# When GpSimd makes the activation sums of the first feed-forward: four blocks at the hidden factors, or six portions after the additions

## The chip, the cores and the metric

One core of one Trainium2 chip runs the program. The metric is device time in microseconds. A core has TensorE (matmuls into PSUM), VectorE, ScalarE, GpSimd and SyncE (here it issues the DMAs); they run their own instruction streams and wait for each other by semaphores.

## The reference

One layer of a diffusion backbone on 1152 tokens (1024 latent and 128 context), width 1024: a half-step SwiGLU feed-forward, a token mixer, and a second feed-forward, each modulated and closed by a layer norm. The change is in the first feed-forward:

```python
def swiglu(h, w_up, w_down):
    a, u = jnp.split(h @ w_up, 2, axis=-1)
    return (jax.nn.silu(a) * u) @ w_down
...
x = layer_norm(ALPHA * x + 0.5 * g1 * swiglu(x * (1.0 + sc1) + sh1, w_f1_in, w_f1_out), ln_g[0], ln_b[0])
```

`w_up` is 1024 x 5632, `w_down` 2816 x 1024, all in float32. The modulation of the later sub-layers (`silu(c) @ w_mod + b_mod`) is worked out beside this feed-forward.

## The kernel before

**Tiling.** The hidden width of 2816 is 22 blocks of 128, taken in 11 groups of two. Every float32 operand is split in two float16 parts, hi and lo, and a product is three matmuls (`PASSES`). For group i TensorE makes six up-projections (`up(i, b, c)`: block b, token chunk c of 384, 48 matmuls each), and between the third and the fourth of them it makes the down-projection of the group before (`down(i - 1)`: 9 token tiles by 2 halves of 512 columns, 6 matmuls each). The down-projection goes through three PSUM banks, which VectorE empties by adding into Y (`add`, 18 additions in a group, counted by the semaphore `y_added`, which begins at 3).

**VectorE's order in a group** (`first_group` of the vector block): the maximum of a weight block; three modulation steps (`mod.steps`, L379, a multiply and sum over a 128 x 1024 tile); `product(i, par, 0, 0)`; `hidden_scale(i - 1)`, whose last instruction L2779 writes the hidden factor and raises `h_scale`; the scale of a weight block; `hidden_lo` (L2787, six pieces of h_lo); `win_lo` (L2730); two steps; two more products; `win_scale`; then the nine tiles of `add(i - 1, t)`, each followed by a step; then `win_lo(2i + 2)`, `wout_scale`, `product(i, par, 1, 0)`, `wout_lo` (L2755, two), two steps, a product, `win_max`, two steps, a product, `hidden_max`. At the end of group 4 it also works over the finished modulation columns (`late_columns`); groups 5 and 6 have a short late scale ahead of the additions. At the end of group 6 `halve_gates` lets TensorE turn the gates into rows (`turn_rows`, L333), ahead of group 7.

**ScalarE** makes the hi parts: after `gate(i, 0, 2)` stands `win_hi(2i + 2)`, and behind it `gate(i, 1, 0)` (the silu of the fourth up-projection) and `wout_hi`.

**Groups 7 and 8** are made otherwise: a product of half size is saved by sums of the activations and of the weights (class `Quarters`). GpSimd makes both. `Quarters.sums(gp, k, late)` makes the activation sums of one k out of four: 17 instructions on tiles of 128 x 576, each waiting for the one before (`link`), into places that stay as they are until group 8. Before the change GpSimd begins with k when `h_scale` has reached k + 2, so one block of 17 runs from the hidden factor in each of the groups 2, 3, 4 and 5. Then come the weight sums (`weight_sums`, L2036, L2039, L2042), one set for each of the blocks 14 to 17. Those of block 14 wait for its load, which SyncE issues when group 5 has split block 12 and its place is free. `win_hi(14)`, on ScalarE in group 6, waits for them (`w_summed`), since L2042 writes into the raw weights; `win_lo(14)` on VectorE (`quarter_lo`, L2722 and L2718), the first instruction after group 6's additions, waits for ScalarE. TensorE asks for the activation sums (`quarters.made`) from the fifth product of group 7 on.

Of the kernel before, what the change touches and what calls it, by code (L numbers as in the profile page):

```python
# [71 lines left out]
class Plan:  # L72


    def __init__(self, nc, base):
        self.nc, self.at = nc, base
# [1451 lines left out]
class MixOut:  # L1528
# [151 lines left out]
    def sums(self, dve, t):  # L1680

        nc, Y = self.nc, self.K.Y
        dve.wait_ge(self.y_taken, 2 * t + 2)
        nc.vector.tensor_tensor(Y[:, t, :], Y[:, t, :], self.xs[t % 2][:], ALU.add).then_inc(self.res_used, 1)
        dve.wait_ge(self.res_used, t + 1)
        if t:
            dve.wait_ge(self.bn, t)
        for half in range(2):
            self.link(nc.vector.bn_stats(self.st[:, half, :], Y[:, t, half * 512:(half + 1) * 512]))
        nc.vector.bn_aggr(self.mv[:, t, :], self.st[:]).then_inc(self.bn, 1)  # L1690
# [250 lines left out]
class Quarters:  # L1941
# [3 lines left out]
    ORDER = ((1, 0), (1, 1), (2, 0), (2, 1), (6, 0), (6, 1), (5, 0), (7, 0), (5, 1), (7, 1), (4, 0), (3, 0), (4, 1), (3, 1))  # L1945
    PER = len(ORDER)
    TMP = 4 * 3 * HALF

    def __init__(self, K, nc, tag, first_group, end_group, spots, staging_at, late_tmp_at, parts_at):
        self.K, self.nc = K, nc  # L1950
# [39 lines left out]

        return self.PER * self.number(blk) + self.at[p, c] + 1

    def sums(self, gp, k, late):

        nc, K, H = self.nc, self.K, self.HALF
        t0, t1, t2 = (t[:] for t in self.tmp[late])
        hi, lo = K.A

        def link(ins):
            self.steps += 1  # L2000
            ins.then_inc(self.summed, 1)
            gp.wait_ge(self.summed, self.steps)

        def add(out, a, b):
            link(nc.gpsimd.tensor_tensor(out, a, b, ALU.add))

        def take(out, a, b):
            link(nc.gpsimd.tensor_tensor(out, a, b, ALU.subtract))

        def split(j, k, x):  # L2010
            link(nc.gpsimd.tensor_copy(self.S[j][0][k][:], x))
            take(self.S[j][1][k][:], x, self.S[j][0][k][:])

        add(t0, hi[:, k, H:], lo[:, k, H:])
        add(t1, hi[:, self.KH + k, H:], lo[:, self.KH + k, H:])
        take(t1, t1, t0)
        split(1, k, t1)
        add(t2, hi[:, k, 0:H], lo[:, k, 0:H])
        take(t0, t2, t0)
        split(3, k, t0)  # L2020
        add(t1, t1, t2)
        link(nc.gpsimd.tensor_scalar(t0, t1, -1.0, None, ALU.mult))
        split(2, k, t0)
        add(t2, hi[:, self.KH + k, 0:H], lo[:, self.KH + k, 0:H])
        take(t1, t1, t2)
        split(4, k, t1)
        gp.sem_inc(self.made, 1)

    def weight_sums(self, gp, blk, raw, raw_in, w_max, in_lo):

        nc, n = self.nc, self.number(blk)
        four = raw[:].rearrange("p s (h k) n -> p (s h) (k n)", h=2)
        gp.wait_ge(raw_in, 32 * (blk // 2) + 32)
        if n:
            gp.wait_ge(in_lo, blk)
        nc.gpsimd.tensor_tensor(self.staged[:, 0:3:2, :], four[:, 0:4:3, :], four[:, 2:3, :].broadcast_to([P, 2, self.KH * P]),  # L2036
                                ALU.add).then_inc(self.w_chain, 1)
        gp.wait_ge(self.w_chain, 2 * n + 1)
        nc.gpsimd.tensor_tensor(self.staged[:, 1, :], four[:, 3, :], self.staged[:, 0, :], ALU.add).then_inc(self.w_chain, 1)  # L2039
        gp.wait_ge(self.w_chain, 2 * n + 2)  # L2040
        gp.wait_ge(w_max, blk + 1)
        nc.gpsimd.tensor_tensor(four[:, 2, :], self.staged[:, 1, :], four[:, 1, :], ALU.add).then_inc(self.w_summed, 1)  # L2042
# [17 lines left out]
def ffn_phase(nc, K, place, banks, tag, w_in, w_out, unit_i, first=False, out_dst=None):  # L2060

    with ExitStack() as ctx:
# [22 lines left out]
        if first:  # L2085
# [3 lines left out]
            quarters = Quarters(K, nc, tag, 7, 9, ((sums_at, sums_at + 36864), (at + 6144, at + 8448)), tmp_at, tmp_at,  # L2089
                                (tmp_at + 6144, at))  # L2090
# [3 lines left out]
        else:  # L2094
            end = Ending(K, nc, tag, place, 2, 8, out_dst, spare_at)
            mix = MixOut(K, nc, place, banks, wout_at, odd_at, odd_at + 4 * GB * TOK, end.gated_at, end.gated_at - 8192)
            quarters = Quarters(K, nc, tag, 3, NG - 1, ((end.gated_at + 12288, end.gated_at + 16384), (end.rows_at, end.rows_at + 8192),
                                                              (mix.free_at + 16384, nc.sbuf_usable_end), (mix.free_at, mix.free_at + 8192), (mix.free_at + 8192, mix.free_at + 16384)),
                                spare_at, spare_at, (end.gated_at, end.gated_at + 6144))
# [8 lines left out]
        h_max, h_spread, h_scale = sem("h_max"), sem("h_max_spread"), sem("h_scaled")  # L2108
        y_ready, y_added, chain = sem("y_ready"), sem("y_added"), sem("chain")
# [4 lines left out]
        HPG = 2 * NT  # L2114
# [579 lines left out]
        def _(dve):  # L2694
# [19 lines left out]
            def quarter_lo(blk, sums):  # L2714
                q, par = quarters, blk % 2
                if sums:
                    dve.wait_ge(q.w_hi, q.number(blk) + 1)
                    nc.vector.scalar_tensor_tensor(q.parts[par][1][:], q.staged[:], ws[:, par:par + 1], q.parts[par][0][:],  # L2718
                                                   ALU.mult, ALU.subtract).then_inc(in_lo, 1)
                else:  # L2720
                    dve.wait_ge(in_hi, blk + 1)
                    nc.vector.scalar_tensor_tensor(win[par][1][:], wraw[par][:], ws[:, par:par + 1], win[par][0][:], ALU.mult, ALU.subtract)  # L2722
# [400 lines left out]
        @block.gpsimd  # L3123
        def _(gp):
            if mod:
                mod.constants(gp)
                weight_sums = lambda blk: quarters.weight_sums(gp, blk, wraw[blk % 2], raw_in[blk % 2], w_max, in_lo)
                gp.wait_ge(mod.feed.lo, NCH * KT)
                for k in range(quarters.KH):
                    gp.wait_ge(h_scale, k + 2)  # L3130
                    quarters.sums(gp, k, False)
                for blk in range(quarters.first_block, quarters.first_block + quarters.blocks):
                    weight_sums(blk)
                gp.wait_ge(quarters.products, quarters.PER * quarters.blocks)
                qkv.pool(gp)
                att.pool(gp)
            else:
                K.tail.root(gp)
                mix.pool(gp)
                gp.wait_ge(mix.feeds[0].lo, 2 * KT)  # L3140
                gp.wait_ge(mix.feeds[1].lo, KT)
                for k in range(quarters.KH):
                    if k == quarters.KH - 1:
                        gp.wait_ge(mix.y_taken, 2 * NT)
                    quarters.sums(gp, k, False)
                gp.wait_ge(mix.scaled_rows, 2)
                for blk in range(quarters.first_block, GB * (NG - 1)):
                    quarters.weight_sums(gp, blk, wraw[blk % 2], raw_in[blk % 2], w_max, in_lo)
                    n = 3 * ((blk - quarters.first_block) // GB)
                    if n < pieces.COUNT:  # L3150
                        pieces.affine(gp, *((n + 1, n + 2) if blk % 2 else (n,)))
                end.pool(gp, y_added, (NG - 2) * HPG + 3)
# [6 lines left out]
def hgrn_phase(nc, K, place, banks):  # L3159

    with ExitStack() as ctx:
# [33 lines left out]
        (raw_in, w_hi, w_lo, acc_p, left, lbs, ready, head) = (  # L3195
            sem(n) for n in ("w_loaded", "w_hi", "w_lo", "projected", "left_psum", "lb_ready", "consts_ready", "head_cols"))
        (logf, sums, sums_e, dev, e_dev, factors) = (
            sem(n) for n in ("logf", "sums", "sums_exp", "deviation", "deviation_exp", "factors"))
        (kt_s, kb_s, a_s, am_s, u_s, st_s, o_s, oe_s) = (
# [348 lines left out]
        def _(act):  # L3548
# [39 lines left out]
            def exps(h, d):  # L3588
                if h >= HGH:
                    return  # L3590
                act.wait_ge(sums, h * 2 + d + 1)
                act.wait_ge(dev, h * 2 + d + 1)
                nc.scalar.activation(sc[d][:, 0:2], sc[d][:, 0:2], ACT.Exp).then_inc(sums_e, 1)
                nc.scalar.activation(B[d][1][:], B[d][2][:], ACT.Exp)
                nc.scalar.activation(B[d][3][:], B[d][2][:], ACT.Exp, scale=-1.0).then_inc(e_dev, 1)
# [480 lines left out]
```

## Time and profile before

| what | us |
|---|---|
| median of 3 runs | 2565.09 (2560.96 to 2565.7) |
| the profiled execution | 2565.44 |
| its span | 2563.5 |
| TensorE busy (matmul) | 2371.9, 93% |
| VectorE busy | 1971.5, 77% |
| ScalarE busy | 893.3, 35% |
| GpSimd busy | 586.2, 23% |
| sums of activations, first feed-forward | 68 instructions, in four blocks of 17, from 196.0 to 464.3 |

Times in rows are microseconds from the span's start. A row of the window view has the window, its length, then the busy time (and count of instructions) of TensorE, its weight loads, VectorE, ScalarE and GpSimd, the granted clock, the share of the DMA engines and GB/s; where it was asked for one engine it has only that engine's busy time. A row of the timeline has start, duration, engine, line, operation, output and inputs, shape and count (instructions of one kind in a row are merged, and the duration is that of all). A group of matmuls overlaps the next one, so TensorE's busy time shows where it stands still, and not how near it is to its peak. The granted clock is the share of full speed that TensorE was allowed: 1.00 is 2.4 GHz, 0.50 is 1.2 GHz. Idle time ahead of an instruction stands in square brackets with what ended it.

### The profile page before, as it was taken

Reading aid. Unit: us, or ns where it says so; the run is one execution under the profiler, and the core shown is the slowest. Engines: PE = TensorE matmul, PEld = TensorE weight load, DVE = VectorE, ACT = ScalarE, POOL = GpSimd, SP = SyncE. Lnnn points to the kernel's source line nnn. Section 1 sums busy time; section 2 is a strip of 40 time slices with the busy share of each in tenths; the row PEclk is TensorE's granted clock in tenths of the full one; section 3 lists DMA queues with packets and bytes.
Section 4 is the critical chain, followed back from the end, with each engine's and each line's share of the span. In section 5 each row is a group of like instructions: output and inputs, shape, how many; then the busy total and the mean of one; then the engine's idle time right before and its main releaser. Section 6 shows DMA issues by size and latency. Waiting matters only on the chain. (4 is left out here: it accounts for less than half of the span.)

```text
span 2563.5 us, 39197 instructions
## 1 busy us (share of the span) xinstructions
PE 2371.9 (93%) x15794; PEld 1515.1 (59%) x15794; DVE 1971.5 (77%) x3043; ACT 893.3 (35%) x1463; POOL 586.2 (23%) x460
## 2 busy tenths in 40 slices
PE   7999999899999787999879999889999999999987
PEld 2554455456655376777757766545555666666643
DVE  3789988996767865788857778888766777877787
ACT  2511111022322244777744544623312333333221
POOL 0004441300100022222210100321862322332047
PEclk9999999899999898999989999899999999999998
DMA  8233232330132210000011101043211222222112
GB/s 312 75 115 103 87 99 91 115 99 18 50 99 71 74 62 3 25 1 1 17 49 38 47 22 61 10 133 117 80 46 58 75 75 74 74 69 69 51 57 99
DMA packets 159702, 181.02 MB, mean 71 GB/s; under 512 B 13144, under 2 KB 129828, under 8 KB 158500
## 3 DMA queue, kind: packets, MB, share of 16 engines
q1 hardware_dynamic: 159524, 178.53, 21.7%
q8 instruction: 126, 2.06, 0.3%
q14 instruction: 52, 0.43, 0.1%
HBM read 158.94 MB, written 19.56 MB: 70 GB/s over the span
## 5 line engine op out<-in xcount | busy, mean ns | idle before, releaser
L2243 PE MATMUL psum<-act_hi,ffn_win_hi 128*128 128x384 f16 x1200 | 391.2, 326 | 4.0 <-DVE ffn_win_lo L2730 2.4
L2243 PE MATMUL psum<-act_hi,ffn_win_lo 128*128 128x384 f16 x1200 | 391.2, 326 | 0.0
L2243 PE MATMUL psum<-act_lo,ffn_win_hi 128*128 128x384 f16 x1200 | 391.2, 326 | 0.0
L2289 PE MATMUL psum<-ffn_wout_hi,ffn_h_hi 128*128 128x512 f16 x720 | 279.9, 389 | 35.9 <-DVE Y L2798 32.5
L2798 DVE SCALAR_TENSOR_TENSOR Y<-psum,ffn_h_unit,Y 128x512 f32<-128x512 f32 x306 | 223.2, 748 | 76.0 <-PE psum L2289 75.1
L2289 PE MATMUL psum<-ffn_wout_lo,ffn_h_hi 128*128 128x512 f16 x720 | 279.4, 388 | 0.0
L2289 PE MATMUL psum<-ffn_wout_hi,ffn_h_lo 128*128 128x512 f16 x720 | 278.9, 387 | 0.0
L2514 ACT ACTIVATE ffn_silu<-psum,ffn_win_inverse 128x384 f32<-128x384 f32 x78 | 45.2, 579 | 623.1 <-PE psum L2243 620.5
L2243 PEld LDWEIGHTS psum<-act_hi,ffn_win_hi 128*128 128x128 f16 x1200 | 117.4, 98 | 81.7 <-DVE ffn_win_lo L2730 2.8
L2243 PEld LDWEIGHTS psum<-act_hi,ffn_win_lo 128*128 128x128 f16 x1200 | 117.4, 98 | 77.6
L2243 PEld LDWEIGHTS psum<-act_lo,ffn_win_hi 128*128 128x128 f16 x1200 | 117.4, 98 | 77.0
L2489 ACT ACTIVATE ffn_win_hi<-ffn_win_raw,ffn_win_scale 128x2048 f16<-128x2048 f32 x44 | 87.8, 1995 | 213.1 <-DVE ffn_win_inverse L2710 104.7
L2289 PEld LDWEIGHTS psum<-ffn_wout_hi,ffn_h_hi 128*128 128x128 f16 x720 | 71.7, 100 | 134.1 <-DVE Y L2798 48.8
L3415 PE MATMUL psum<-act_hi,scan_w_hi 128*128 128x384 f16 x384 | 125.4, 326 | 0.0
L3415 PE MATMUL psum<-act_lo,scan_w_hi 128*128 128x384 f16 x384 | 125.2, 326 | 0.0
L3415 PE MATMUL psum<-act_hi,scan_w_lo 128*128 128x384 f16 x384 | 125.2, 326 | 0.0
L2289 PEld LDWEIGHTS psum<-ffn_wout_hi,ffn_h_lo 128*128 128x128 f16 x720 | 71.8, 100 | 89.2 <-issue 7.4
L2336 PE MATMUL psum<-act_lo,ffn_win_hi 128*128 128x288 f16 x432 | 124.4, 288 | 0.0
L2336 PE MATMUL psum<-act_hi,ffn_win_lo 128*128 128x288 f16 x432 | 124.3, 288 | 0.0
L2336 PE MATMUL psum<-act_hi,ffn_win_hi 128*128 128x288 f16 x432 | 124.3, 288 | 0.0
L2336 PE MATMUL psum<-ffn_a_sum_hi,ffn_w_sums_hi 128*128 128x288 f16 x432 | 123.6, 286 | 0.0
L2336 PE MATMUL psum<-ffn_a_sum_lo,ffn_w_sums_hi 128*128 128x288 f16 x432 | 123.6, 286 | 0.0
(427 smaller groups left out, 5811.2 us busy)
## 6 DMA issues: line engine op xcount, KB each, us to landing
ffn_win_raw<-in_w_in SPq DMA_DIRECT2D x88, 512.0 KB, 5.1
w_mod_columns<-in_w_mod_columns SPq DMA_DIRECT2D x56, 512.0 KB, 3.2
ffn_wout_raw<-in_w_out SPq DMA_DIRECT2D x44, 512.0 KB, 4.5
scan_w_raw<-in_w_mix SPq DMA_DIRECT2D x20, 512.0 KB, 4.5
x_after<-Y SPq DMA_DIRECT2D x18, 512.0 KB, 5.3
w_mod<-in_w_mod SPq DMA_DIRECT2D x8, 1024.0 KB, 10.0
mixout_residual<-x_after SPq DMA_DIRECT2D x9, 512.0 KB, 3.4
residual_piece<-x_after SPq DMA_DIRECT2D x18, 256.0 KB, 2.7
```

The lines of the kernel that those rows point to most:

```text
L2243: last = nc.tensor.matmul(bank[:, 0:CH], win[b][w][:, half, k, :], K.A[a][:, k, c * CH:(c + 1) * CH], start=(n == 0), stop=(n == 3 * KT - 1))
L2289: last = nc.tensor.matmul(py[m % 3], h[a][:, b, t * P:(t + 1) * P], wout[w][:, b, 0, half * 512:(half + 1) * 512], start=(n == 0), stop=(n ...
L2336: last = nc.tensor.matmul(X if p in (1, 6, 7, 4) else Yb, lhs, rhs, start=(p in (1, 2, 5) and m == 0), stop=(m == 3 * q.KH - 1), skip_grou ...
L2489: nc.scalar.activation(win[par][0][:], wraw[par][:], ACT.Copy, scale=ws[:, par:par + 1]).then_inc(in_hi, 1)
L2514: nc.scalar.activation(sa[s][:], pa[s][:, 0:CH], ACT.Silu, scale=winv[:, b:b + 1]).then_inc(silu, 1)
L2798: ins = nc.vector.scalar_tensor_tensor(dst, py[m % 3], hq[:], dst, ALU.mult, ALU.add)
L3415: last = nc.tensor.matmul(proj[u % 2][:, 0:CH], w[x][:, k, :], K.A[y][:, k, i * CH:(i + 1) * CH], start=(m == 0), stop=(m == 3 * KT - 1))
```

## The change

`sums` gets a function `pace`, called after every twelfth instruction of all 68, with a running number. The wait for the hidden factor is gone. In its place GpSimd waits for `y_added` of 1 x 18 + 3 ahead of the first instruction, which is when group 1's additions are done, and after instruction 12n for the end of group n + 1's additions. So there are portions of 12, 12, 12, 12, 12 and 8, begun after the additions of groups 1 to 6. The instructions and their order stay. The second feed-forward gives no `pace`. The weight sums stay behind all the activation sums in GpSimd's stream.

```diff
@@ class Quarters
+    PACE = 12
...
-    def sums(self, gp, k, late):
+    def sums(self, gp, k, late, pace=None):
...
         def link(ins):
             self.steps += 1
             ins.then_inc(self.summed, 1)
             gp.wait_ge(self.summed, self.steps)
+            if pace is not None and self.steps % self.PACE == 0:
+                pace(self.steps // self.PACE)
@@ ffn_phase, gpsimd block
                 gp.wait_ge(mod.feed.lo, NCH * KT)
+                added = lambda i: gp.wait_ge(y_added, i * HPG + 3)
+                added(1)
                 for k in range(quarters.KH):
-                    gp.wait_ge(h_scale, k + 2)
-                    quarters.sums(gp, k, False)
+                    quarters.sums(gp, k, False, lambda n: added(n + 1))
                 for blk in range(quarters.first_block, quarters.first_block + quarters.blocks):
                     weight_sums(blk)
```

## Rows read from the trace of the kernel before

**Rows 1.** Busy time by window, from one hidden factor to the next, groups 1 to 6
```profile
124.85:195.62 70.77, 70.77 (x404) 39.48 (x402) 61.92 (x101) 12.60 (x16) 0.00 (x0) 1.00 0.34 112
195.62:274.73 79.11, 73.87 (x404) 40.18 (x402) 71.36 (x101) 12.60 (x16) 26.91 (x17) 0.96 0.31 100
274.73:353.50 78.77, 73.61 (x404) 40.05 (x402) 71.28 (x102) 12.60 (x16) 26.91 (x17) 0.96 0.31 100
353.50:436.81 83.31, 78.16 (x433) 42.94 (x431) 75.08 (x123) 12.60 (x16) 26.91 (x17) 0.96 0.29 96
436.81:517.99 81.18, 70.22 (x383) 38.00 (x381) 76.20 (x106) 12.49 (x16) 33.59 (x20) 0.92 0.31 98
517.99:591.21 73.22, 69.47 (x400) 39.70 (x399) 61.94 (x104) 15.33 (x20) 5.89 (x3) 0.98 0.25 80
```

**Rows 2.** The same view of VectorE: us, busy, granted clock, DMA share, GB/s
```profile
124.85:141.09 16.24, 12.44 (x27) 1.00 0.33 98
195.62:217.34 21.72, 21.06 (x26) 1.00 0.24 73
436.81:459.80 22.99, 22.04 (x31) 0.85 0.23 69
```

**Rows 3.** Timeline of VectorE, group 1: start, us, line, what, idle before
```profile
126.21 3.26 DVE L2787 SCALAR_TENSOR_TENSOR ffn_h_lo<-ffn_h_even,ffn_h_factor,ffn_h_hi 128x384 f16<-128x384 f32 x6
...
132.45 1.28 DVE L379 CUSTOM_DVE_ANT_0 w_mod_columns<-w_mod_columns,silu_cond_rows,param_cols 128x1024 f32<-128x1024 f32 x1
...
138.75 0.62 DVE L2763 SCALAR_TENSOR_TENSOR ffn_h_odd<-psum,ffn_win_inverse,ffn_silu 128x384 f32<-128x384 f32 x1 [2.46 <-ACT ffn_silu L2514]
```

**Rows 4.** Timeline of VectorE, group 3
```profile
276.37 9.12 DVE L2787 SCALAR_TENSOR_TENSOR ffn_h_lo<-ffn_h_even,ffn_h_factor,ffn_h_hi 128x384 f16<-128x384 f32 x6
...
288.08 2.29 DVE L379 CUSTOM_DVE_ANT_0 w_mod_columns<-w_mod_columns,silu_cond_rows,param_cols 128x1024 f32<-128x1024 f32 x1
...
292.64 0.61 DVE L2763 SCALAR_TENSOR_TENSOR ffn_h_odd<-psum,ffn_win_inverse,ffn_silu 128x384 f32<-128x384 f32 x1
```

**Rows 5.** Timeline of TensorE, group 2
```profile
218.15 0.61 PE L2289 MATMUL psum<-ffn_wout_hi,ffn_h_hi 128*128 128x512 f16 x1 [5.24 <-DVE Y L2798]
```

**Rows 6.** VectorE by window, additions' end to next group, groups 1 and 6
```profile
163.80:193.48 29.68, 24.84 (x35) 1.00 0.40 127
557.37:581.41 24.04, 21.71 (x32) 1.00 0.29 88
```

**Rows 7.** Timeline of VectorE: the wout_lo of groups 2 and 5
```profile
250.36 2.48 DVE L2755 SCALAR_TENSOR_TENSOR ffn_wout_lo<-ffn_wout_raw,ffn_wout_scale,ffn_wout_hi 128x1024 f16<-128x1024 f32 x2
...
492.76 4.64 DVE L2755 SCALAR_TENSOR_TENSOR ffn_wout_lo<-ffn_wout_raw,ffn_wout_scale,ffn_wout_hi 128x1024 f16<-128x1024 f32 x2
```

**Rows 8.** Timeline of GpSimd; below, two lines' durations, ns min/median/max
```profile
451.43 2.26 POOL L2005 TENSOR_TENSOR ffn_a_sum_tmp_early<-ffn_a_sum_tmp_early,ffn_a_sum_tmp_early 128x576 f32<-128x576 f32 x1
...
463.01 1.28 POOL L2008 TENSOR_TENSOR ffn_a_sum_lo<-ffn_a_sum_tmp_early,ffn_a_sum_hi 128x576 f16<-128x576 f32 x1
...
611.38 2.40 POOL L2036 TENSOR_TENSOR ffn_w_sums<-ffn_win_raw 128x1024 f32<-128x1024 f32 x1 [34.21 <-DVE ffn_w_sums_lo L2718]
...
615.23 1.27 POOL L2042 TENSOR_TENSOR ffn_win_raw<-ffn_w_sums,ffn_win_raw 128x512 f32<-128x512 f32 x1
...
L2022 POOL TENSOR_SCALAR fn_a_sum_tmp_early<-fn_a_sum_tmp_early x4: 1649/1677/2502, 1814.7 to 1888.0; 128x576 f32<-128x576 f32 x4
...
L2005 POOL TENSOR_TENSOR fn_a_sum_tmp_early<-fn_a_sum_tmp_early,fn_a_sum_tmp_early x4: 1399/1402/1408, 1813.2 to 1886.5; 128x576 f32<-128x576 f32 x4
```

**Rows 9.** Timeline of ScalarE, groups 6 and 7
```profile
535.27 1.56 ACT L2491 ACTIVATE ffn_w_sums_hi<-ffn_w_sums,ffn_win_scale 128x1536 f16<-128x1536 f32 x1
...
616.61 2.00 ACT L2489 ACTIVATE ffn_win_hi<-ffn_win_raw,ffn_win_scale 128x2048 f16<-128x2048 f32 x1 [11.84 <-POOL ffn_win_raw L2042]
```

**Rows 10.** Timeline of VectorE and TensorE at the end of group 6
```profile
557.37 2.34 DVE L2722 SCALAR_TENSOR_TENSOR ffn_win_lo<-ffn_win_raw,ffn_win_scale,ffn_win_hi 128x2048 f16<-128x2048 f32 x1
...
581.39 0.81 PE L333 MATMUL psum<-ident,mod_cols 128*8 128x128 f32 x6 [2.93 <-DVEq L390]
```

## Prediction

> **What bounds the kernel now.** I read the trace of the first feed-forward group by group, since the edit touches only GpSimd's sums there. First the busy time in six windows, each from one group's hidden factor (VectorE, L2779) to the next; I call them groups 1 to 6 [rows 1]. The reader is to see that group 1, in which GpSimd does nothing, takes 70.77 us with TensorE busy in all of it, and that groups 2 to 5, each with one block of 17 GpSimd instructions (20 in the last, with two of the weight sums), take 79.11, 78.77, 83.31 and 81.18. The work of TensorE is the same in each; in these four it stands still for some 5 to 11 us, and its granted clock is 0.96 or 0.92 and not 1.00.
>
> Then where in the group the time goes. From the hidden factor to the first addition into Y VectorE takes 16.24 us in group 1, 3.8 of it idle, and 21.72 us in group 2 with no idle time but the 0.66 of gaps between its instructions [rows 2]. Between lie six h_lo, one win_lo, two modulation steps (L379), two products and a scale. In group 1 VectorE waits 2.46 us for the third product's silu: TensorE ends last there [rows 3]. In group 3 the same six h_lo take 9.12 us and not 3.26, a step 2.29 and not 1.28 [rows 3, 4]: these read two SBUF tensors while GpSimd's sums run beside them. So the additions begin late, the three PSUM banks of the output sums are full, and TensorE waits 5.24 us [rows 5]. What ends last is VectorE in groups 2 to 5, slowed by GpSimd, and TensorE in group 1.
>
> **What goes: the block at the hidden factor.** The sums no longer begin with the hidden factor but when the 18 additions of a group are done. Groups 2 to 5 then have group 1's course. Group 2 falls from 79.11 to 70.77: 8.3. Group 3: 8.0. Group 4 holds the late columns too, which I price by its surplus over group 3, 83.31 - 78.77 = 4.5; what remains is 8.0. Group 5 begins with VectorE some 4.5 us behind for these columns, so the idle 2.46 of group 1 isn't there and TensorE still waits a little. Its stretch from factor to first addition, 22.99 us, has a late scale in it, 22.99 - 21.72 = 1.3. Without GpSimd it would be 16.24 - 2.46 + 1.3 = 15.1: 7.9 less. Sum: 8.3 + 8.0 + 8.0 + 7.9 = 32.2 us [rows 1 to 3]. The lower bound is the earlier start of the additions alone, 4 x 5.5 = 22, if TensorE gave back nothing after it.
>
> **What comes: portions after the additions in groups 1 to 5.** 17 instructions for each of four k are 68; the pace fires at 12, 24, 36, 48 and 60, so there are five portions of 12 and one of 8, begun after the additions of groups 1 to 6. Of 17 instructions in 26.9 us of a contended group [rows 1], 12 make 19 us. Beside them VectorE runs: win_lo, two wout_max, a product, two wout_lo, two steps, a product, a win_max, two steps, a product. A product, with one operand in PSUM, took 0.61 us beside GpSimd and 0.62 alone [rows 3, 4]; reductions, with one operand, I take as untouched too, since h_lo and steps already make up nearly all that group 3 lost. What stretches is win_lo, the wout_lo and the steps. The pair of wout_lo took 4.64 us beside GpSimd and 2.48 alone, 1.08 each [rows 7]; a step 1.0 more [rows 3, 4]. In 19 us stand win_lo (0.4, an estimate: a long one loses less), two wout_lo (2.2), two steps (2.0) and perhaps one of the next two (1.0): 5.6 us. Bounds: nothing below zero, since nothing is removed here, and 8 us, if all seven pay 1.08. Against that, from the additions' end to the next group's first product, VectorE is busy 24.84 of 29.68 us in group 1, where TensorE ends last; less 0.66 for gaps that is 4.2 us of waiting [rows 2, 6]. So 1.4 us is left, and it comes to the next hidden factor; in groups 2, 3, 4 and 6 the 2.46 us of idle before the third product covers it [rows 3]. Only in group 5, where the late columns have used that cover, does it count: 1.4.
>
> The Trainium skill (SBUF — State Buffer, on the shared port pair) has it that VectorE and GpSimd hold that port as an exclusive lock for a whole instruction and the loser blocks fully, that a VectorE instruction with two SBUF inputs contends with a GpSimd one that reads SBUF, and that tensor_reduce never does. The trace agrees on who is slowed. It doesn't quite on how much: an h_lo lost 9.12/6 - 3.26/6 = 0.98 us, less than the 1.40 of a GpSimd f32 add alone [rows 3, 4, 8]. By the row the late time is 1.4 us a group, by a full block 5.6, which is a rival below.
>
> **What comes: the last portion and the weight sums in group 6.** This is the edit's price. Before, GpSimd was free by group 5, and made the sums of block 14's weights as soon as they had landed, so that ScalarE could round them (535.27) under the additions [rows 9]. Now eight activation steps stand ahead of them in GpSimd's queue, and these begin only with the last addition of group 6. The eight took 12.9 us contended (451.43 to 464.29) [rows 8]; here VectorE will soon stand, and the one negation falls from 2.5 to 1.68, the f32 add from 2.26 to 1.40, so I take 10.7, between 10 and 12.9. Then the three weight sums, 611.38 to 616.50, 5.1 us [rows 8]. I count from the end of the step behind the last addition; that addition ends some 1.1 us earlier (a step is 1.28), so the sums are ready at -1.1 + 0.2 + 10.7 + 5.2 = 15.0.
>
> Behind that wait: ScalarE's win_hi of block 14 (L2489, 2.0 us; in group 7 it waits 11.84 us for just such a sum) and its sums' part (1.56), and behind them gate(6, 1, 0) and wout_hi; VectorE's win_lo (L2722), first thing after the additions, and behind it wout_scale, the product, wout_lo, four steps, the block maximum and halve_gates [rows 9, 10]. win_lo starts at 15.0 + 0.1 + 2.0 = 17.1, not 0. TensorE goes on with up(6, 1, 0) and (6, 1, 1), 15.6 us of work, then waits about 11 us for the product, and starts again at a lower clock (0.92 over group 5, with its long wait) [rows 1]; even so VectorE is later. VectorE has 17.1 us lost, and recovers only the waiting it had, 24.04 - 21.71 - 0.7 = 1.6 us [rows 6], but meets GpSimd in one step more or less as now: at halve_gates it is 15.5 to 16 us late, and TensorE's turn_rows (L333), which already now waits 2.93 us for it, goes with it [rows 10]. I take 15.8; bounds 11 (only TensorE's wait) and 19 (contended steps, 12.9).
>
> Loads: the columns of all remaining steps are issued ahead of SyncE's wait for block 14's split. Behind it stands only block 16's load, issued at about 21 us and needed at about 40. Nothing else is moved on a queue. Blocks 15 to 17 have their sums in the order of before.
>
> **Sum.** The profiled execution took 2565.44 us, its span 2563.5. 2565.4 - 32.2 + 1.4 + 15.8 = 2550.4. The median of before, 2565.09, lies 0.35 lower, so I leave the forecast at 2550.4. All of it lies ahead of group 7; later phases shift as a whole.
>
> **Rivals.**
> First, full blocks. Each of the seven contending instructions waits out a whole GpSimd add, 1.40 us: 9.8 us, less 4.2 of idle, 5.6 late per group. Groups 2, 3, 4 and 6 cover 2.5 of it and lose 3.1, group 5 loses all: 18.0. 2565.4 - 32.2 + 18.0 + 15.8 = 2567.0, no measurable change. For it: two streams of reads through one port. Against: 0.98 and 1.08 a piece in the rows. The rule of the Trainium skill's page above would have it come out this way.
>
> Second, slower: a portion outlasts the idle times. If GpSimd, stretched itself by VectorE, needs 30 us and not 19 for twelve instructions, it runs into the three steps after the last product too, and into both before it. Five steps at 1.0 come on the 1.4: 6.4 late. Less 2.5 where there is cover: 3.9 x 4 + 6.4 = 22.0. 2565.4 - 32.2 + 22.0 + 15.8 = 2571.0. It decides from the point at which a portion ends more than 24 us after the additions. Against: while VectorE reduces or waits, GpSimd runs at its own pace.
>
> Third, faster: group 6 costs less, since the eight go at their shortest and VectorE has nothing to catch up behind turn_rows: 11 instead of 15.8, and group 5's 1.4 is covered as well: 2565.4 - 32.2 + 11 = 2544.2.
>
> Fourth, only the additions' start is gained (22 for 32.2): 2560.6. Against it stands group 1's whole length. That the sums don't move, or that two portions run together, would need GpSimd to be at work for a whole group; that is part of the second.
>
> **Chances.** Forecast 0.61 (its own range 2546 to 2556), full blocks 0.10, outlasting 0.08, cheaper group 6 0.12, additions' start alone 0.09. A measurement here can tell 0.2% (5 us) from no change: faster is below 2560.0, slower above 2570.2. Faster: 0.61 + 0.12 + half of the fourth and some of the first, 0.80; same 0.12; slower 0.08. The range, 2543 to 2563, leaves out the two rivals above it.
>
> **What would show it.** Group 2 to 4 at 71 to 72 us from hidden factor to hidden factor, with granted clock 1.00, six h_lo in 3.3 us, and no wait of TensorE for Y. wout_lo pairs of about 4.6 us and first steps of 2.2 after the additions in groups 1 to 5; a portion's end about 20 us after the additions. In group 6 a wait of ScalarE for GpSimd's L2042 and of VectorE before L2722 of some 17 us, TensorE idle about 11 us ahead of up(6, 1, 2), and group 6 at 89 us. It is wrong if h_lo is still stretched, if product(i, 0, 0) comes over 2.5 us behind its silu in groups 2 to 4, or if group 6 stays under 80 us.

## Result: 2565.2 us before, 2551.2 us after

| | before | after |
|---|---|---|
| median | 2565.20 (2560.96 to 2565.7, 4 runs) | 2551.18 (2548.43 to 2552.7, 4 runs) |
| ratio | | 0.9948 [0.9931, 0.9965] |
| profiled execution, span | 2565.44, 2563.5 | 2548.43, 2546.6 |
| TensorE's waits, 100 to 620 us | 27.6 for additions, 2.9 at L333 | 4.5 for additions, 11.8 for a product, 4.1 at L333 |
| groups 1 to 6 | 466.4 | 449.2 |

The kernel is faster by 14 us between the medians and by 17.0 between the profiled executions. Lines of the class and of the feed-forward stand three further down than before (L2787 is L2790, L2798 is L2801, L2722 is L2725, L2489 is L2492); L379 and L333 are the same.

All of the difference between the two profiles lies in groups 2 to 6. This is the window view of the kernel after, from one hidden factor to the next, columns as in [rows 1]:

```profile
124.90:195.67 70.77, 70.77 (x404) 39.52 (x402) 65.68 (x102) 12.71 (x16) 20.61 (x12) 1.00 0.35 112
195.67:267.60 71.93, 71.93 (x412) 40.21 (x409) 67.08 (x101) 12.71 (x16) 20.69 (x12) 1.00 0.34 110
267.60:337.87 70.27, 70.27 (x400) 39.19 (x399) 66.34 (x102) 12.48 (x16) 21.50 (x12) 1.00 0.35 113
337.87:412.95 75.08, 75.08 (x431) 42.12 (x429) 70.02 (x124) 12.60 (x16) 19.68 (x12) 1.00 0.33 106
412.95:484.69 71.74, 68.38 (x379) 37.33 (x378) 68.36 (x107) 12.59 (x16) 20.18 (x12) 0.98 0.34 110
484.69:574.11 89.42, 72.73 (x402) 40.76 (x401) 61.85 (x104) 15.09 (x20) 21.29 (x14) 0.90 0.21 65
```

Groups 2 and 3 are back at about group 1's length, group 4 at 4.3 us more (the late columns are worked out there), all three at a granted clock of 1.00: against [rows 1] they lose 7.2, 8.5 and 8.2 us, group 5 loses 9.4, and group 6 gains 16.2, with the clock down from 0.98 to 0.90. Together 17.1 us.

What brought groups 2 to 5 down is seen in VectorE's timeline of the kernel after. Two rows from group 2, one from group 3:

```profile
197.02 3.26 DVE L2790 SCALAR_TENSOR_TENSOR ffn_h_lo<-ffn_h_odd,ffn_h_factor,ffn_h_hi 128x384 f16<-128x384 f32 x6
...
209.57 0.62 DVE L2766 SCALAR_TENSOR_TENSOR ffn_h_even<-psum,ffn_win_inverse,ffn_silu 128x384 f32<-128x384 f32 x1 [2.46 <-ACT ffn_silu L2517]
...
280.35 0.62 DVE L2766 SCALAR_TENSOR_TENSOR ffn_h_odd<-psum,ffn_win_inverse,ffn_silu 128x384 f32<-128x384 f32 x1 [1.30 <-ACT ffn_silu L2517]
```

The six h_lo take 3.26 us and not 9.12 [rows 4], and the idle time ahead of the third product is there again, 2.46 us as in group 1 [rows 3]. In group 3 1.30 us of it are left: the portion in group 2 brought the next hidden factor 1.2 us late (group 2 takes 71.93 us, group 1 70.77), and the idle time takes that up. Over GpSimd's first portion, at the end of group 1, the same view of VectorE shows what a portion costs:

```profile
163.84 3.35 DVE L2733 SCALAR_TENSOR_TENSOR ffn_win_lo<-ffn_win_raw,ffn_win_scale,ffn_win_hi 128x2048 f16<-128x2048 f32 x1
...
171.56 3.66 DVE L2758 SCALAR_TENSOR_TENSOR ffn_wout_lo<-ffn_wout_raw,ffn_wout_scale,ffn_wout_hi 128x1024 f16<-128x1024 f32 x2 [0.21 <-ACT ffn_wout_hi L2499]
...
175.14 2.42 DVE L379 CUSTOM_DVE_ANT_0 mod_product<-w_mod_columns,silu_cond_rows,param_cols 128x1024 bf16<-128x1024 f32 x1
...
177.60 1.56 DVE L379 CUSTOM_DVE_ANT_0 w_mod_columns<-w_mod_columns,silu_cond_rows,param_cols 128x1024 f32<-128x1024 f32 x1
...
185.66 0.62 DVE L2766 SCALAR_TENSOR_TENSOR ffn_h_odd<-psum,ffn_win_inverse,ffn_silu 128x384 f32<-128x384 f32 x1 [0.25 <-ACT ffn_silu L2517]
```

win_lo takes 3.35 us (2.35 alone), the two wout_lo 3.66 (2.48 alone), the first two steps 2.42 and 1.56 (1.28 alone), the next two 1.28 and 1.56 again. GpSimd's portion runs to 184.3. The product is not late: it still waits 0.25 us for its silu.

Group 6 shows the price. GpSimd's timeline of the kernel after, then ScalarE's, VectorE's and TensorE's:

```profile
523.43 2.31 POOL L2008 TENSOR_TENSOR ffn_a_sum_tmp_early<-ffn_a_sum_tmp_early,ffn_a_sum_tmp_early 128x576 f32<-128x576 f32 x1 [51.28 <-DVE Y L2801]
...
534.65 2.37 POOL L2039 TENSOR_TENSOR ffn_w_sums<-ffn_win_raw 128x1024 f32<-128x1024 f32 x1 [0.18 <-POOL ffn_a_sum_lo L2011]
...
538.47 1.26 POOL L2045 TENSOR_TENSOR ffn_win_raw<-ffn_w_sums,ffn_win_raw 128x512 f32<-128x512 f32 x1
```

```profile
539.83 2.00 ACT L2492 ACTIVATE ffn_win_hi<-ffn_win_raw,ffn_win_scale 128x2048 f16<-128x2048 f32 x1 [41.86 <-POOL ffn_win_raw L2045]
...
541.86 2.35 DVE L2725 SCALAR_TENSOR_TENSOR ffn_win_lo<-ffn_win_raw,ffn_win_scale,ffn_win_hi 128x2048 f16<-128x2048 f32 x1 [17.37 <-ACT ffn_win_hi L2492]
...
549.50 0.50 PE L2246 MATMUL psum<-act_hi,ffn_win_hi 128*128 128x384 f16 x1 [11.80 <-DVE ffn_h_even L2766]
...
564.29 0.81 PE L333 MATMUL psum<-ident,mod_cols 128*8 128x128 f32 x6 [4.07 <-DVEq L390]
```

GpSimd begins its last eight activation sums at 523.43, with the additions' end, and the weight sums at 534.65. ScalarE has waited 41.86 us for them, VectorE's win_lo 17.37 for ScalarE, and TensorE 11.80 for VectorE's product. TensorE then starts at half clock. The window view of TensorE alone (us, busy, granted clock, DMA share, GB/s), after that wait and after the wait at L333:

```profile
549.50:554.92 5.42, 5.42 (x18) 0.50 0.48 126
564.29:568.60 4.31, 4.31 (x23) 0.62 0.03 6
564.29:575.10 10.81, 10.81 (x76) 0.84 0.01 2
```

Before the change TensorE waited 5 to 11 us for additions in four groups [rows 5], now it waits 11.8 us once.

### The profile page after: what moved, and what is told of

Read it like the earlier page. It is cut to its first block and busy times, and to the rows that moved or that the text cites. A ratio compares the mean times of both kernels' runs of the same rounds, so it can differ in the third digit from the quotient of the medians.

```text
span 2546.6 us, 39202 instructions
## 1 busy us (share of the span) xinstructions
PE 2364.7 (93%) x15794; PEld 1514.0 (59%) x15794; DVE 1955.4 (77%) x3043; ACT 892.8 (35%) x1463; POOL 589.0 (23%) x460
## 5 line engine op out<-in xcount | busy, mean ns | idle before, releaser
L2246 PE MATMUL psum<-act_hi,ffn_win_hi 128*128 128x384 f16 x1200 | 392.4, 327 | 15.8 <-DVE ffn_h_even L2766 11.8
L2801 DVE SCALAR_TENSOR_TENSOR Y<-psum,ffn_h_unit,Y 128x512 f32<-128x512 f32 x306 | 221.5, 747 | 70.4 <-PE psum L2292 69.4
L2492 ACT ACTIVATE ffn_win_hi<-ffn_win_raw,ffn_win_scale 128x2048 f16<-128x2048 f32 x44 | 87.8, 1995 | 228.8 <-POOL ffn_win_raw L2045 124.3
L2339 PE MATMUL psum<-ffn_a_sum_hi,ffn_w_sums_lo 128*128 128x288 f16 x432 | 123.6, 286 | 0.0
```

Source lines behind the costliest of these rows:

```text
L2246: last = nc.tensor.matmul(bank[:, 0:CH], win[b][w][:, half, k, :], K.A[a][:, k, c * CH:(c + 1) * CH], start=(n == 0), stop=(n == 3 * KT - 1))
L2339: last = nc.tensor.matmul(X if p in (1, 6, 7, 4) else Yb, lhs, rhs, start=(p in (1, 2, 5) and m == 0), stop=(m == 3 * q.KH - 1), skip_grou ...
L2492: nc.scalar.activation(win[par][0][:], wraw[par][:], ACT.Copy, scale=ws[:, par:par + 1]).then_inc(in_hi, 1)
L2801: ins = nc.vector.scalar_tensor_tensor(dst, py[m % 3], hq[:], dst, ALU.mult, ALU.add)
```

## Experiments

All are compared with the kernel before, on the same chip: 2565.18 us (2564.07 to 2566.94, 13 runs) for the first four and 2566.72 (2562.1 to 2566.89, 7 runs) for the last two. Diffs are against the kernel after, but for that of no_sums. The table has the distance between hidden factors, group by group.

| kernel | g1 | g2 | g3 | g4 | g5 | g6 | sum | median | ratio |
|---|---|---|---|---|---|---|---|---|---|
| before | 70.8 | 79.1 | 78.8 | 83.3 | 81.2 | 73.2 | 466.4 | 2565.2 | |
| after | 70.8 | 71.9 | 70.3 | 75.1 | 71.7 | 89.4 | 449.2 | 2551.18 | 0.9948 [0.9931, 0.9965] |
| at_the_factor | 78.6 | 78.5 | 76.1 | 82.2 | 78.6 | 76.8 | 470.8 | 2569.81 | 1.0018 [1.0009, 1.0028] |
| four_portions | 72.5 | 70.8 | 70.8 | 76.9 | 72.1 | 73.1 | 436.2 | 2535.57 | 0.9886 [0.9872, 0.9901] |
| five_portions | 71.4 | 72.0 | 71.1 | 74.9 | 73.4 | 72.8 | 435.5 | 2533.93 | 0.988 [0.9865, 0.9895] |
| no_sums | 70.8 | 70.8 | 70.8 | 75.5 | 72.1 | 73.2 | 433.2 | 2530.52 | 0.987 [0.9855, 0.9885] |
| five_then_late_sums | 71.4 | 72.0 | 71.1 | 74.9 | 72.0 | 81.1 | 442.5 | 2540.83 | 0.9906 [0.989, 0.9923] |
| after_again | 70.8 | 71.9 | 70.3 | 75.1 | 71.6 | 89.4 | 449.0 | 2547.94 | 0.9935 [0.992, 0.995] |

### at_the_factor: portions of twelve, but at the hidden factors

```diff
-                added = lambda i: gp.wait_ge(y_added, i * HPG + 3)
+                added = lambda i: gp.wait_ge(h_scale, i)
```

> The six portions of the change, but begun at the hidden factor of groups 1 to 6 and not after the additions. If the place is what the change brings, twelve instructions beside six h_lo, win_lo and a step cost VectorE about 7 us a group, 2.5 of it covered, and what TensorE loses after it: about 7 us in each of five groups and 5 in the sixth, 40 us against the 32 of before: 2573 us (2566 to 2578). If spreading the work in smaller portions is what helps, it is faster than before, 2555 us or less. In group 6 the weight sums come about 4 us after ScalarE could first take them, hidden under the additions.

Measured: 2569.81 us (2567.73 to 2571.49), 0.2% slower than before. The window view of groups 2 and 5, then VectorE's timeline and TensorE's of group 2:

```profile
201.13:279.62 78.49, 73.56 (x404) 40.11 (x402) 70.91 (x101) 12.61 (x16) 19.21 (x12) 0.96 0.31 101
...
437.92:516.49 78.57, 67.78 (x377) 37.15 (x375) 71.94 (x107) 12.50 (x16) 18.59 (x12) 0.93 0.30 101
```

```profile
202.84 8.98 DVE L2790 SCALAR_TENSOR_TENSOR ffn_h_lo<-ffn_h_odd,ffn_h_factor,ffn_h_hi 128x384 f16<-128x384 f32 x6
...
223.35 0.61 PE L2292 MATMUL psum<-ffn_wout_hi,ffn_h_hi 128*128 128x512 f16 x1 [4.93 <-DVE Y L2801]
```

With 12 instructions at the factor and not 17, the six h_lo take 8.98 us and TensorE waits 4.93 us, nearly what it waited before [rows 5]. Groups 2 to 5 are 315.4 us together, 289.0 in the kernel after: with portions of the same size, their place is worth 26 us over these four groups. The other 7 us to the kernel before (322.4) go with the shorter portion; in group 5 the sums of block 14 have moved too, so that they are not its price alone. Group 1 now pays as well, 7.8 us, which takes that back, and group 6 makes it slower than before. Group 6 is only 3.6 us longer, since the last eight sums begin with its hidden factor, 38 us earlier in the group: the 16.2 us of the kernel after come from the place of the last portion too.

### no_sums: what the sums cost where they are

Eight GpSimd memsets of a k's tiles stand at the hidden factor of groups 2 to 5, as in the kernel before; they only write. The activation sums are left out. The diff is against the kernel before.

```diff
+    def blank(self, gp, k):
+        for j in (1, 2, 3, 4):
+            for a in range(2):
+                self.steps += 1
+                self.nc.gpsimd.memset(self.S[j][a][k][:], 0.0).then_inc(self.summed, 1)
+                gp.wait_ge(self.summed, self.steps)
+        gp.sem_inc(self.made, 1)
...
                 for k in range(quarters.KH):
                     gp.wait_ge(h_scale, k + 2)
-                    quarters.sums(gp, k, False)
+                    quarters.blank(gp, k)
```

> Leaves out the activation sums of the first feed-forward: in their place GpSimd sets the 32 tiles to zero, eight memsets at the hidden factor of groups 2 to 5, which write and read nothing in SBUF; the weight sums as before. This is the floor for the cost of the sums. My theory: all of the 32 to 33 us of before come from the sums' reads beside VectorE's two-input reads: 2532 us (2530 to 2535), groups 2 and 3 at 70.8 us, h_lo at 0.54 us although the memsets run beside them. Rival: part of it is the wait for the hidden factor or the writes: 2540 us or more, h_lo over 0.7 us. The rule of the Trainium skill (SBUF - State Buffer, on the shared port pair) is that a GpSimd instruction that only writes doesn't contend with VectorE's second read, which gives the first of the two.

Measured: 2530.52 us (2530.49 to 2533.44). Windows of groups 2 and 5, then (L2796 is L2790) one row each of GpSimd's and VectorE's timeline in group 2:

```profile
195.45:266.23 70.78, 70.78 (x404) 39.52 (x402) 61.94 (x102) 12.62 (x16) 4.63 (x8) 1.00 0.35 112
...
412.48:484.61 72.13, 69.02 (x383) 37.74 (x381) 67.31 (x106) 12.50 (x16) 11.33 (x11) 0.98 0.34 110
```

```profile
198.35 0.58 POOL L1998 MEMSET ffn_a_sum_hi<- 128x576 f16 x1
...
196.81 3.26 DVE L2796 SCALAR_TENSOR_TENSOR ffn_h_lo<-ffn_h_odd,ffn_h_factor,ffn_h_hi 128x384 f16<-128x384 f32 x6
```

Without the sums groups 2 to 5 take 289.2 us, in the kernel after 289.0. Groups 2 to 4 can be compared as they stand, 217.0 us here and 217.3 after: the portions stretch VectorE (67.08 us busy in group 2 after, 61.94 here) and make single hidden factors up to 1.2 us late, but next to nothing is left of it by the end of group 4. In group 5 (72.1 and 71.7) no_sums has the sums of block 14 beside VectorE's end, as before, and the kernel after a portion instead, so there the portion alone has no price from this pair. The blocks at the factor cost 322.4 - 289.2 = 33.2 us. The memsets leave out two things at once, the reads and most of GpSimd's time (4.63 us of work for 26.91); what bears on the reads alone is that the six h_lo, with memsets beside all of them (195.81 to 200.84), took 3.26 us. Between the kernel after and this one lie 449.2 - 433.2 = 16.0 us in groups 1 to 6, all of it in group 6, 15.0 between the profiled executions (2548.43 and 2533.44), and 20.7 between the medians (17.4 with the second measurement of the kernel after, below). What the medians have beyond group 6 was not located.

### five_portions and four_portions: no portion left for group 6

Fourteen to a portion leave 12 for the fifth, so that the three sums of block 14 can follow in group 5 (15 instructions there in the window); seventeen make four portions (the wait after the last of them is on group 5's additions, ahead of the weight sums).

```diff
-    PACE = 12
+    PACE = 14
```

and 17 for the other.

> PACE is 14 and not 12: portions of 14, 14, 14, 14 and 12 after the additions of groups 1 to 5, none in group 6. My theory: the 17 us that VectorE waits in group 6 go away whole, since the weight sums of block 14 are made at the end of group 5 again, and two more instructions a portion cost next to nothing: 2551 - 16 = 2535 us (2532 to 2539), group 6 at 73 to 74 us. Rival, full blocks or a portion that outlasts the idle times: the longer portions push the hidden factors later by 2 us or more in each of five groups, 2541 us or more. Rival, group 6 would have waited anyway (for TensorE or for halve_gates): 2547 us or more.

> PACE is 17: four whole blocks of 17, as before the change, but after the additions of groups 1 to 4; the weight sums begin with the end of group 5's additions. It tells the place from the size. If the place alone matters: as with five portions, 2536 us (2532 to 2541), h_lo at 0.54 us each. If it is the small size of a portion that hides it, a block of 17 (22 to 27 us) reaches into the steps before the hidden factor, VectorE comes 3 to 5 us late there, and with 2.5 us of cover some 2 us are lost in each of groups 2 to 5: 2544 us.

Measured: 2533.93 us (2532.31 to 2535.32) and 2535.57 (2535.1 to 2535.74). The window view of five_portions, groups 1, 5 and 6, and then of four_portions, groups 1, 2 and 4:

```profile
123.70:195.12 71.42, 71.42 (x408) 39.90 (x406) 66.34 (x101) 12.73 (x16) 24.02 (x14) 1.00 0.34 111
...
413.07:486.42 73.35, 68.67 (x375) 37.26 (x374) 69.01 (x107) 12.62 (x16) 27.57 (x15) 0.95 0.33 108
...
486.42:559.19 72.77, 69.01 (x398) 39.40 (x396) 61.95 (x103) 15.34 (x20) 5.89 (x3) 0.98 0.25 80
```

```profile
124.76:197.25 72.49, 72.49 (x415) 40.56 (x413) 67.40 (x101) 12.73 (x16) 27.37 (x17) 1.00 0.34 109
...
197.25:268.03 70.78, 70.78 (x404) 39.53 (x403) 67.40 (x102) 12.62 (x16) 27.36 (x17) 1.00 0.35 112
...
338.80:415.74 76.94, 75.91 (x434) 42.41 (x433) 72.70 (x123) 12.62 (x16) 27.41 (x17) 1.00 0.32 103
```

Group 6 is back at 72.8 us, 16.6 less than in the kernel after, and the gain of groups 2 to 5 stays. GpSimd's 14 instructions take 24 us and still fit, but for 0.6 us in group 1; its 17 take 27.4 and make the hidden factor of group 1's end 1.7 us late, and of group 4's another 1.5 (76.94 and 75.48 in no_sums). In groups 2 and 3 the idle time takes up the lateness that they begin with, and they end with as much. Five portions are 31 us faster than before and 3.4 us from the kernel without the sums. Between five and four portions lie 1.6 us, and their runs overlap (2532.31 to 2535.32, 2535.1 to 2535.74), so that which is faster is not shown.

### five_then_late_sums: only the weight sums late

Is it the wait for the sums of block 14 that costs in group 6, or that the eight activation sums run beside VectorE's work there? Here all activation sums are done by group 5, and the weight sums alone begin with the end of group 6's additions.

```diff
-    PACE = 12
+    PACE = 14
...
                     quarters.sums(gp, k, False, lambda n: added(n + 1))
+                added(6)
                 for blk in range(quarters.first_block, quarters.first_block + quarters.blocks):
```

> Five portions, and GpSimd waits for the end of group 6's additions before the weight sums of block 14: of the queue in group 6 only the three weight sums are left, without the eight activation instructions ahead of them. My theory: each microsecond that GpSimd's L2045 is late after the additions comes through to turn_rows, less the 1.6 us of waiting in VectorE's rest of the group. The sums are ready at -1.1 + 0.2 + 5.2 = 4.3 us, win_lo starts at 6.4, halve_gates is 4.8 us late: 2533.9 + 4.8 = 2538.7 us (2537 to 2541), VectorE's wait before L2725 about 6.3 us and not 17.4. Rival: below 13 us of lateness TensorE's two up-projections hide it (15.6 us of work), only the clock and the long wait cost: 2534 us.

Measured: 2540.83 us (2539.89 to 2541.62). GpSimd's, VectorE's and TensorE's timeline in group 6, and below VectorE's win_lo in five_portions:

```profile
524.15 3.36 POOL L2039 TENSOR_TENSOR ffn_w_sums<-ffn_win_raw 128x1024 f32<-128x1024 f32 x1 [50.53 <-DVE Y L2801]
...
528.94 1.27 POOL L2045 TENSOR_TENSOR ffn_win_raw<-ffn_w_sums,ffn_win_raw 128x512 f32<-128x512 f32 x1
...
532.34 2.35 DVE L2725 SCALAR_TENSOR_TENSOR ffn_win_lo<-ffn_win_raw,ffn_win_scale,ffn_win_hi 128x2048 f16<-128x2048 f32 x1 [7.06 <-ACT ffn_win_hi L2492]
...
539.04 1.26 DVE L2746 TENSOR_SCALAR ffn_wout_unit<-ffn_wout_unit 128x2 f32<-128x2 f32 x1
...
555.85 1.44 PE L333 MATMUL psum<-ident,mod_cols 128*8 128x128 f32 x6 [6.81 <-DVEq L390]
```

```profile
525.35 2.35 DVE L2725 SCALAR_TENSOR_TENSOR ffn_win_lo<-ffn_win_raw,ffn_win_scale,ffn_win_hi 128x2048 f16<-128x2048 f32 x1
```

GpSimd's three sums end at 530.2, 6.1 us after the additions, and win_lo waits 7.06. Group 6 is 8.3 us longer than in five_portions, and group 5, out of which the sums of block 14 have gone, 1.4 shorter: 7.0 together, 6.9 between the medians. The 1.4 us of group 5 are not kept. The hidden factor comes at 484.95 and not 486.42, but group 6's additions are behind VectorE at 525.28 (win_lo's start less its wait) and 525.35. So the whole loss stands behind the additions, where group 6 still takes 40.78 us (to 566.06) and not 33.84 (to 559.19): 6.9 us. It is 2 us more than expected: win_lo started 7.0 us later than in five_portions and not 6.4. Not foreseen was that a row of 128 x 2 numbers (L2746, 0.17 us alone) took 1.26 us, from 539.04 to 540.30, beside a GpSimd sum from 539.01 to 540.27. Another 0.4 us went behind halve_gates (10.78 us to the next hidden factor and not 10.39). TensorE waited 6.8 us at L333 and not 2.9.

So it is the wait for the weight sums that costs, and not the activation sums: counted from the additions' end to the next hidden factor, a wait of 7.06 us cost 6.9, and one of 17.37 in the kernel after 15.8 (49.62 against 33.84 before). Of the eight activation sums all but the first ran while VectorE stood waiting, from 524.49 on.

### after_again: the kernel after once more, unchanged

> The changed kernel unaltered, on the chip and in the rounds of the kernel beside it, and with a second profile. The profiled execution took 2548.43 us, the median 2551.18, and the forecast was made from one profile of before at 2565.44. If the 2.6 us between them lie in the stretch that the forecast is about, the hidden factors of groups 1 to 7 come at other times in the second profile (spill of the portions that varies); if they lie elsewhere, these times agree within 1 us relative to the first and the difference is behind group 7. I expect 2551 us (2548 to 2553) and the second.

Measured: 2547.94 us (2546.97 to 2550.85). Its windows of groups 5 and 6:

```profile
411.81:483.37 71.56, 68.23 (x379) 37.32 (x378) 68.35 (x107) 12.60 (x16) 20.19 (x12) 0.98 0.34 111
483.37:572.77 89.40, 72.65 (x402) 40.74 (x401) 61.82 (x104) 15.09 (x20) 21.29 (x14) 0.90 0.21 65
```

Each group agrees with the first profile within 0.2 us, so the steps' sizes are repeatable. Both profiles are of executions at the fast end (2548.43 and 2547.04), so where the executions of 2551 to 2553 us lose is not shown.

## Why the prediction was right

Forecast 2550.4 us, measured 2551.18, inside the range of 2543 to 2563 and faster, as the case with the most chance had it. That it came within 1 us is luck: by the profiles group 5 came out 3 us better than its term, and the median of the kernel after lies 2.8 us above its profiled execution, while that of before lies 0.2 below. By its steps, each against the two profiles:

| step | forecast | measured |
|---|---|---|
| groups 2, 3, 4: block at the factor goes | -24.3 | -23.9 |
| group 5, factor to first addition | -7.9 | -7.9 |
| group 5, the rest (the portion's lateness) | +1.4 | -1.6 |
| group 6 | +15.8 | +16.2 |
| sum | -15.0 | -17.1 |

**The block at the factor** was sized from group 1 as a control, and that is borne out twice: the rows of the kernel after, and no_sums, which has 33.2 us for the four groups where 32.2 was forecast. In group 5 the first addition came 15.10 us after the hidden factor (412.95 to 428.05), forecast 15.1. at_the_factor shows that it is the place that counts. The rival "additions' start only" (22 us) falls with it: groups 2 and 3 return to group 1's length, and groups 2 to 4 to its clock.

**The portions beside the end of a group** were forecast to take 5.6 us of VectorE, by single prices taken from the rows. By VectorE's busy time it is 65.68 - 61.92 = 3.8 us in group 1, 67.08 - 61.94 = 5.1 in group 2 and 66.34 - 61.94 = 4.4 in group 3, under the forecast each time, and not in the parts forecast: in group 1 win_lo lost 1.0 and not 0.4, the wout_lo pair 1.2 and not 2.2, the steps 1.7 and not 3.0. The pair had been priced beside GpSimd's long weight sums [rows 7], not beside the activation sums that it meets now. The lateness at a hidden factor, 1.4 us forecast each time, was none behind group 1 and 1.2 behind group 2, and the idle time of the next group covered it, as the step had it. The rival of full blocks (9.8 us a portion, 2567.0) is refuted by these same rows: no single two-input VectorE instruction beside GpSimd's portions lost more than 1.2 us. The Trainium skill's rule (SBUF — State Buffer, the shared port pair) is borne out on who meets among the two-input instructions and the reductions: L127's kept their 2.46 and 2.29 us beside the portions. On the size the measured rows decide. "A portion outlasts the idle times" (30 us instead of 19) didn't happen: the first took 21.5 us from its first instruction (162.87 to 184.3). four_portions is where it begins.

**Group 5** is the term that was wrong in sign. Behind the first addition +1.4 us was forecast and -1.6 measured. The rows split it, before and then after: TensorE's wait for additions, and TensorE's windows from the first addition to VectorE's win_lo and from there to the next hidden factor.

```profile
460.61 0.61 PE L2289 MATMUL psum<-ffn_wout_hi,ffn_h_hi 128*128 128x512 f16 x1 [10.96 <-DVE Y L2798]
459.80:484.98 25.18, 24.37 (x103) 0.87 0.25 84
484.98:517.99 33.01, 33.01 (x207) 1.00 0.41 128
```

```profile
428.86 0.61 PE L2292 MATMUL psum<-ffn_wout_hi,ffn_h_hi 128*128 128x512 f16 x1 [3.36 <-DVE Y L2801]
428.05:452.01 23.96, 23.15 (x103) 0.93 0.26 88
452.01:484.69 32.68, 32.68 (x205) 1.00 0.40 129
```

1.2 us were gained among the additions: TensorE comes to them from a wait of 3.36 us and not 10.96, and its granted clock over that stretch is 0.93 and not 0.87. The forecast counted only up to the first addition. The end of the group changed by -0.3 us where it had +1.4. The lateness itself was there, but small: the last product ahead of the factor started 0.6 us behind its silu (482.55, silu's end 481.92). Before the change it started 1.0 behind (515.86 and 514.89); a step ahead of it (512.33) had taken 2.16 us and not 1.28, beside the last of the three sums of block 14 (511.25 to 513.42; the prediction counts two of them). These sums are gone from there, and the forecast counted what they cost in group 6 and not what they leave in group 5. five_portions and five_then_late_sums put that at 73.35 - 71.98 = 1.4 us beside a portion, which the next group did not keep.

**Group 6** came out by its steps: sums ready 15.3 us after the additions (15.0 forecast), win_lo 17.4 (17.1), TensorE's wait 11.8 (about 11), halve_gates 15.5 to 16 late, forecast from 17.1 less the 1.6 of idle time before. From the additions' end on the group is 15.8 us longer, as forecast; the other 0.4 of the 16.2 lies ahead of it (39.80 us against 39.38). The way from win_lo to halve_gates took 21.85 us (541.86 to 563.71) and before 23.44: 1.6 recovered. The rival of a cheaper group 6 (11 us) fails on just that: VectorE, not TensorE, ends last. five_portions and five_then_late_sums show that this whole term can be taken away without giving up the rest.

The net of the profiles is 2 us better than forecast, the difference of the medians 1 us worse; both lie inside what a measurement can tell. Runs of the kernel after scatter from 2547 to 2552.7; its groups 1 to 6 repeat to 0.2 us in the two profiles, both of fast executions. Where the scatter lies was not followed up.

## What to carry to other kernels

Work of a side engine that slows the bound one belongs where that one waits anyway; read from a group without it both the price and the room, and size the portions to the room (here 14 instructions fitted in 24 us, 17 in 27 did not quite). Then count what is queued behind it: a last portion of eight sums, 11 us long, stood ahead of three that the critical chain needed, and gave back half of what the move had brought. Where something moves out of a stretch, price both ends, and follow what it gives back as far as the next engine that waits anyway: here 1.4 us at a hidden factor were gone 40 us later, at the additions' end.

## What the runs showed of the hardware

As expected, memsets on GpSimd cost VectorE nothing: six h_lo took 3.26 us beside them, against 9.12 beside the sums [rows 4]. Not expected was that a tiny VectorE instruction can lose as much as a large one: a tensor_scalar of 128 x 2 (L2746) took 1.26 us and not 0.17, and in the kernel after another (L2745, 128 x 2, int32) took 0.84 in group 4 and 0.94 in group 5, against 0.17 in group 6 and 0.23 in groups 1 to 3. After a wait of 11.8 us TensorE ran 5.4 us at a granted clock of 0.50, that is 1.2 GHz; after 4.07 us of waiting at L333 it ran at 0.84 over the next 10.8 us, 0.62 in the first 4.3.
